# Splitting the inverse products of two chunked mixers over four quadrants of TensorE

## The reference

```python
# gated_delta_chunked, per head and direction, c = 64
a_mat = beta[..., :, None] * jnp.einsum('nhcid,nhcjd->nhcij', k, k) * d_strict
rhs = jnp.concatenate([beta[..., None] * v, (beta * gam)[..., None] * k], axis=-1)
sol = lax.linalg.triangular_solve(a_mat, rhs, left_side=True, lower=True, unit_diagonal=True)
u0, w = sol[..., :dv], sol[..., dv:]
```

## Time and profile before

| | |
|---|---|
| median of 3 runs | 1995.14 us |
| all runs | 2004.53, 1994.45, 1995.14 us |
| span of the profiled execution | 2001.2 us |
| PE busy | 1764.2 us (88%) |
| DVE busy | 857.6 us (43%) |
| ACT busy | 592.7 us (30%) |
| L525 MATMUL (all `product` calls) | 215.5 us busy, 6656 instructions |

### The profile page before, as it was taken

How to read it: one execution, slowest core, us unless ns; L and a number is a source line. 1 busy time by engine, 2 the same in 40 slices (tenths; PEclk the granted TensorE clock), 3 DMA queues, 4 the chain that set the end, 5 groups by cost and what they waited for, 6 DMA issues and landing times.

```text
span 2001.2 us, 44027 instructions
## 1 busy us (share of the span) xinstructions
PE 1764.2 (88%) x17970; PEld 1033.3 (52%) x17970; DVE 857.6 (43%) x1514; ACT 592.7 (30%) x1018; POOL 243.5 (12%) x270
## 2 busy tenths in 40 slices
PE   5998895977778877898999899999989998899996
PEld 2444543544444444445865784354447856853452
DVE  1567524111111111367666753151457747642331
ACT  3314521000000000334324424252253325424442
POOL 0002211111111111006112100001002103000001
PEclk8998996999999999998999999999999999999998
DMA  9758025999999999521000003110211000012101
GB/s 358 259 197 291 1 69 220 370 423 424 423 424 424 425 424 413 216 74 33 3 3 2 3 20 109 42 43 32 80 43 35 3 2 2 4 65 104 42 1 42
DMA packets 75098, 307.75 MB, mean 154 GB/s; under 512 B 10908, under 2 KB 22300, under 8 KB 57888
## 3 DMA queue, kind: packets, MB, share of 16 engines
q1 hardware_dynamic: 63280, 291.98, 37.2%
q0 software_dynamic: 5360, 9.33, 1.3%
q10 hardware_dynamic: 6272, 3.81, 0.6%
HBM read 301.01 MB, written 16.52 MB: 159 GB/s over the span
## 4 chain that ended last, share of the span: by engine, by line
PE 73%; DVE 13%; another core or an unknown queue 6%; ACT 4%; issue 3%; DMA 1%; DVEq 0%; ACTq 0%; POOL 0%; POOLq 0%
PE bank L2253 12%; PE bank L496 12%; PE bank L2269 6%; PE bank L1027 6%; PE bank L525 5%; PE bank L532 4%; PE bank L2091 3%; PE bank L2175 3%; PE bank L998 2%; DVE arena L1596 2%; ACT arena L1039 1%; PE bank L512 1%; PE bank L2115 1%; PE bank L2103 1%
## 5 line engine op out<-in xcount | busy, mean ns | idle before, releaser
L496 PE MATMUL bank<-hT,arena 128*128 128x512 f32 (+1 forms) x640 | 287.7, 605 | 3.6 <-ACTq L1040 2.4
L2253 PE MATMUL bank<-arena 128*64 128x256 f32 x1792 | 216.3, 399 | 66.9 <-remote 66.9
L525 PE MATMUL bank<-arena 64*64 64x64 f32 x6656 | 215.5, 220 | 22.7 <-DVE arena L1726 7.2
L525 PEld LDWEIGHTS bank<-arena 64*64 64x64 f32 x6656 | 203.8, 136 | 37.0 <-DVE arena L1726 10.1
L2253 PEld LDWEIGHTS bank<-arena 128*64 128x64 f32 x1792 | 135.6, 143 | 158.0 <-issue 107.8
L496 PEld LDWEIGHTS bank<-hT,arena 128*128 128x128 f32 (+1 forms) x640 | 122.9, 194 | 161.2 <-issue 156.6
L2859 DVE COPY arena<-bank 128x256 f32<-128x256 f32 x32 | 13.6, 425 | 329.6 <-PE bank L2261 329.6
L2269 PE MATMUL bank<-arena 128*64 128x512 f32 x448 | 104.0, 606 | 16.4 <-remote 16.4
L1027 PE MATMUL bank<-arena 128*128 128x512 f32 x256 | 110.4, 593 | 0.0
L1039 ACT ACTIVATE arena<-bank 128x512 f32<-128x512 f32 (+2 forms) x124 | 73.2, 590 | 118.9 <-PE bank L496 79.2
L532 PE MATMUL bank<-hT,arena 128*128 128x512 f32 x224 | 105.0, 607 | 1.7 <-remote 1.7
(11 more groups left out here) (448 smaller groups left out, 2677.1 us busy)
## 6 DMA issues: line engine op xcount, KB each, us to landing
arena<-w_gate SPq DMA_DIRECT2D x28, 2048.0 KB, 30.6
arena<-w_up SPq DMA_DIRECT2D x28, 2048.0 KB, 21.0
arena<-w_down SPq DMA_DIRECT2D x28, 2048.0 KB, 26.2
arena<-w_ada SPq DMA_DIRECT2D x12, 2048.0 KB, 19.7
arena<-w_in SPq DMA_DIRECT2D x10, 2048.0 KB, 11.7
arena<-w_out SPq DMA_DIRECT2D x6, 2048.0 KB, 7.6
arena<-w_in SPq DMA_DIRECT2D x6, 1536.0 KB, 6.9
hT<-w_up SPq DMA_DIRECT2D x4, 2048.0 KB, 20.9
```

Source lines behind the costliest of these rows:

```text
L496: m = pe.matmul(bank[b][0:w, :], slot2(n)[:, k, c:c + w], hT[:, k, :], start=(k == 0), stop=(k == KD - 1))
L525: m = pe.matmul(o[half(f), s, t], lhs[half(f), s, t], rhs[half(f), s, t], start=True, stop=True)
L2253: mm = pe.matmul(bank[b][c * CAP:(c + 1) * CAP, 0:FE // 2], XT[j][:, k % 4, k // 4, :], e_slot(e_at(e, i), KD)[:, k, c * (FE // 2):(c + 1) ...
```

## The change

The eight matrices of a partition half are now seen as four pairs: `by_parity` splits the 512 columns in 64-column pieces with even (`j=0`) and odd (`j=1`) number, which are even and odd token tiles. Products of even tiles stay as they were. For odd tiles, the first product reads half `f` and writes the *other* half; the second product reads V there, with a copy of Y's odd tiles that ACT has put in that half, and writes back to half `f`. Results of even and odd tiles go to two banks, `2d` and `2d+1`; the first product uses columns 0 to 255 of both, the second columns 256 to 511 (`results`).

```diff
+        Y_odd = [rs[:, 256 * d:256 * d + 256].rearrange("p (a n) -> p a n", n=CG) for d in range(2)]
+        def results(d, part):
+            return banks[:, 2 * d:2 * d + 2, 256 * part:256 * part + 256].rearrange("p j (a n) -> p j a n", n=CG)
+        def by_parity(ap):
+            return ap.rearrange("p (a j n) -> p j a n", j=2, n=CG)
...
+            four = [(j, f) for j in range(2) for f in range(2)]
+            def crossing(o, lhs, rhs):
+                lhs, rhs = by_parity(lhs), by_parity(rhs)
+                for a in range(TT):
+                    for j, f in four:
+                        m = pe.matmul(o[half(f ^ j), j, a], lhs[half(f), j, a], rhs[half(f), j, a], start=True, stop=True)
+                return m
+            def returning(o, Y, Y_odd, V, last):
+                Y, V = by_parity(Y), by_parity(V)
+                for a in range(TT):
+                    for j, f in four:
+                        y = Y_odd[half(1 - f), a] if j else Y[half(f), 0, a]
+                        v = V[half(f ^ j), j, a]
+                        m = pe.matmul(o[half(f), j, a], v if last else y, y if last else v, start=True, stop=True)
+                return m
...
                     for l in range(1, LEVELS):
                         for d in range(2):
+                            if l == 1:
+                                for j in range(2):
+                                    pe.wait_ge(bank_free[2 * d + j], 1)
                             t_full[d].wait()
-                            product(d, g_Bn[d], g_T[d]).then_inc(sem(f"g_v_done{d}"), 1)
+                            crossing(results(d, 0), g_Bn[d], g_T[d]).then_inc(sem(f"g_v_done{d}"), 1)
                         for d in range(2):
                             v_full[d].wait()
-                            y_full[d].wait()
-                            if l == 1:
-                                pe.wait_ge(bank_free[2 + d], 1)
...
+                            y_odd[d].wait(2)
+                            returning(results(d, 1), g_Y[d], Y_odd[d], g_V[d],
+                                      l == LEVELS - 1).then_inc(sem(f"g_t_done{d}"), 1)
...
+            def crossed(y_full, d, l, Y, more=1):
+                z = 1 << l
+                o = (1 if d == 0 else 0) if l < LEVELS - 1 else slice(0, 2)
+                def columns(ap):
+                    return ap.rearrange("p a (g o n) -> p a g o n", o=2, n=z)[:, :, :, o]
+                y_full[d].wait(more)
+                for f in range(2):
+                    act.activation(columns(Y_odd[d][half(1 - f)]), columns(by_parity(Y)[half(f), 1]),
+                                   ACT.Copy).then_inc(sem(f"y_odd_full{d}"), 1)
...
                     for l in range(1, LEVELS):
                         for d in range(2):
+                            if l == 1:
+                                crossed(y_full, d, l, g_Y[d], 2 if ht else 1)
                             v_done[d].wait()
                             if l == 1:
                                 pt_full[d].wait()
-                            act.activation(g_V[d], bank[d], ACT.Copy).then_inc(sem(f"g_v_full{d}"), 1)
+                            act.activation(by_parity(g_V[d]), results(d, 0), ACT.Copy).then_inc(sem(f"g_v_full{d}"), 1)
+                            if l > 1:
+                                crossed(y_full, d, l, g_Y[d])
...
                             if l < LEVELS - 1:
-                                dve.copy_predicated(blocks(g_T[d]), merged(d, l, False), blocks(bank[2 + d])).then_inc(sem(f"g_t_full{d}"), 1)
+                                dve.copy_predicated(by_parity(g_T[d]), merged_parity(d, l, False), results(d, 1)).then_inc(sem(f"g_t_full{d}"), 1)
```

More of the change, by code:

```diff
@@ L542, in decay_rows @@
                         for t, f in pairs_in:
-                            m = pe.matmul(pieces(bank[b + d])[half(f), s, t], g_g[half(f), t, c + s:c + s + 1].to_broadcast([CG, CG]),
+                            m = pe.matmul(pieces(bank[at[d]])[half(f), s, t], g_g[half(f), t, c + s:c + s + 1].to_broadcast([CG, CG]),
                                           const2("cum" + name)[half(f), half(f)], start=True, stop=True)
@@ L565, in gdn_chunks @@
                                                    ("g_t_full", "g_y_full", "g_v_full", "g_uw_free")]
-                rk_full = [Count(pe, sem(f"g_rk_full{d}")) for d in range(2)]
+                rk_full, y_odd = [[Count(pe, sem(f"{n}{d}")) for d in range(2)] for n in ("g_rk_full", "y_odd_full")]
                 kk_free = Count(pe, sem("g_kk_free"))
@@ L694, in rwkv_chunks @@
                 in_full, bt_full, k_free = [Count(pe, sem(n)) for n in ("r_in_full", "r_bt_full", "r_k_free")]
+                y_odd = [Count(pe, sem(f"y_odd_full{d}")) for d in range(2)]
                 for b in range(4, 8):
@@ L1159, in act_second @@
                 w_done = Count(act, sem("g_w_done"))
+                y_full = [Count(act, sem(f"g_y_full{d}")) for d in range(2)]
                 for ht in range(3):
@@ L1166, in act_second @@
                     if ht == 1:
-                        values(2, 3)
+                        values(2, 0)
                         raw(6, 2)
@@ L1262, in act_second @@
                         for d in range(2):
+                            if l == 1:
+                                crossed(y_full, d, l, r_kmt[:, ct, d], 2 if ct else 1)
                             v_done[d].wait()
-                            act.activation(r_kr[:, ct, d, 0], bank[d], ACT.Copy).then_inc(sem(f"g_v_full{d}"), 1)
+                            act.activation(by_parity(r_kr[:, ct, d, 0]), results(d, 0), ACT.Copy).then_inc(sem(f"g_v_full{d}"), 1)
+                            if l > 1:
+                                crossed(y_full, d, l, r_kmt[:, ct, d])
                         if ct == 0 and l in (2, 3):
@@ L1500, in exponents @@
                         e_args[d].wait()
-                        chain(dve.tensor_tensor(pieces(g_V[d]), pieces(bank[b + d]), key_term, ALU.add))
+                        chain(dve.tensor_tensor(pieces(g_V[d]), pieces(bank[at[d]]), key_term, ALU.add))
                         dve.tensor_tensor(blocks(g_V[d]), blocks(g_V[d]), over_blocks(const2("farF" if d == 0 else "farB")),
@@ L1600, in dve_second @@
                             else:
-                                dve.copy_predicated(blocks(g_Y[d]), merged(d, l, True), blocks(bank[2 + d])).then_inc(sem(f"g_y_full{d}"), 1)
+                                dve.copy_predicated(by_parity(g_Y[d]), merged_parity(d, l, True), results(d, 1)).then_inc(sem(f"g_y_full{d}"), 1)
                         if l in (2, 3):
@@ L1725, in dve_second @@
                             if l < LEVELS - 1:
-                                dve.copy_predicated(blocks(Tm), merged(d, l, False), blocks(bank[2 + d])).then_inc(sem(f"g_t_full{d}"), 1)
+                                dve.copy_predicated(by_parity(Tm), merged_parity(d, l, False), results(d, 1)).then_inc(sem(f"g_t_full{d}"), 1)
                                 n_t[d] += 1
@@ L1730, in dve_second @@
                             else:
-                                dve.copy_predicated(blocks(Y), merged(d, l, True), blocks(bank[2 + d])).then_inc(sem(f"g_y_full{d}"), 1)
+                                dve.copy_predicated(by_parity(Y), merged_parity(d, l, True), results(d, 1)).then_inc(sem(f"g_y_full{d}"), 1)
                         if ct == 0 and l in (1, 2):
```

52 lines of the change are left out of this document (24 added, 28 removed).

## The result

The changed kernel takes 2007.45 us (median of 4 runs, 2002.70 to 2010.91) where the kernel before takes 1994.82 in the same comparison: ratio 1.0059, interval 1.0033 to 1.0085. It is slower by 0.6 %. The forecast was 1975, 1967 to 1989.

The account below looks back on a forecast made before the run. PE was taken to bound GDN block 2 and RWKV block 2, DVE RWKV block 1. Levels 8.7 + starts 2.8 - late u 1.6 = 9.9 us a layer, 19.8 for both; 1995.1 - 19.8 = 1975 us, range 1967 to 1989.

Parts of the forecast that it names:

- 2 x 8.7: Levels between first and last merge of five blocks: 8.7 us saved per layer, in two layers.
- The starts: Changed products on four quadrants: matmuls start 14.6 ns apart, so 0.47 us a product.
- The rivals of the floor and of the bank: Products: 25 ns start floor gives 1989 us, shared-bank conflict 1998; 0.14 together with dear copies or DVE.
- crosses Y0 from 2.13: In a new level, ACT copies Y0 across halves from 2.13 to 2.65 us after merge 0.
- The second product of d=0 starts at about 2.75: In a new level, PE starts this product 2.75 us after merge 0; the next merge follows at 3.45.
- a period of 3.45 us: A PE-bound level, merge to merge, falls from 4.29 to 3.45 us.
- a rival for dear copies, 1988 us: ACT's Y copies cost 1.15 us a pair, period about 4.1, forecast time 1988; 0.14 together with floor, bank or DVE.
- No DMA is touched: Listed among things unchanged at no cost: weights for these stages were loaded earlier, and no DMA is touched.
- Starts +2.8: Level 1, ahead of each block's first merge: 2.8 us saved per layer.
- late u -1.6: After the last level, u of d=1 starts 0.4 us later: 1.6 us lost per layer over four blocks.
- The clock, given 0.08: Rival: PE idles between shorter products and its clock falls to half, giving 2015 us; chance 0.08.
- costs little: A clock dip in RWKV's first, DVE-bound block costs little, since PE has over 2 us to spare there.

Follow-up runs that it names:

- e2: Changed kernel without ACT's copies of Y's odd tiles; the second product reads Y in place (result wrong): 1981.14 us, ratio 0.9930.
- e7: Changed kernel with ACT's copies still in its queue, but PE waits only for Y, not for them (result wrong): 1989.75 us, ratio 0.9968.
- e1: Kernel before, products on two quadrants as before, plus ACT's copies of Y's odd tiles and the waits for them: 2023.99 us, ratio 1.0145.
- e9: Changed kernel plus 26 small padding matmuls (104 PE instructions) ahead of each layer's first block: 2003.37 us, ratio 1.0038.
- e5: Changed kernel plus 8 small padding matmuls (32 PE instructions) ahead of each layer's first block: 2022.25 us, ratio 1.0122.
- e12: Changed kernel with 26 padding matmuls a layer, and each block's first level without crossing or copies: 2005.66 us, ratio 1.0046.
- e13: Changed kernel with six blocks' copies on GpSimd, 26 padding matmuls a layer, and first levels without crossing or copies: 2000.04 us, ratio 1.0013.
- e10: Changed kernel with the Y copies of six of ten blocks on GpSimd instead of ACT, plus 26 padding matmuls a layer: 1992.97 us, ratio 0.9984.
- e15: Changed kernel with crossing only in six blocks, copies on GpSimd; the first GDN and first RWKV blocks keep straight products without copies: 1992.35 us, ratio 0.9966.
- e16: Changed kernel with crossing only in six blocks, copies on GpSimd, plus 26 padding matmuls a layer: 1991.40 us, ratio 0.9970.
- e11: Kernel before plus 26 padding matmuls a layer: 2001.26 us, ratio 1.0026.
- e3: Changed kernel plus idle-filling matmuls of 256 columns behind three products of each level from level 2 on: 2007.21 us, ratio 1.0057.
- e6: Changed kernel plus a smaller filler, matmuls of 192 columns behind two products of each level from level 2 on: 2008.58 us, ratio 1.0056.

## Why the prediction was wrong

The miss is 32 us: 1975 forecast, 2007.45 measured. In the spans the levels are 3.5 us longer than in the second profile of the kernel before instead of 17.4 shorter (2 x 8.7), which is 21 us of it; the rest, some 12 us, lies outside them.

- **The starts: right.** The new products' matmuls are 15.4 ns apart (32 in 0.48 us), against 14.6 taken. The shared bank cost nothing, and the 25 ns that the page "TensorE: Matmul & The Clock Gate" of the Trainium skill gives as the least distance is not seen in this pattern either. The rivals of the floor and of the bank fall.
- **"crosses Y0 from 2.13", "The second product of d=0 starts at about 2.75", "a period of 3.45 us": the step that failed, and the one that weighs most.** The sum let the pair of copies end with V1, so that it cost a level nothing: its 3.45 us with copies is no more than e2's 3.42 without. Measured, the product waits for the pair and starts at 3.04 us: V copy to copy 0.63 for 0.50 us, the pair 0.64 for 0.52, to the product 0.14 for 0.10, product to merge 0.75 for 0.70. A clean level is 3.79 us. The pair hardly overlaps: the 0.1 us was taken from V copies of 512 elements. Without copies the run is 26 us faster (e2), and some 18 us of these are the wait for them (e7); on the old products they cost 29 us (e1). The forecast had a rival for dear copies, 1988 us at 1.15 us a pair; the pair was not dear, it stood in the chain.
- **How far this error goes in the levels.** Over the twenty-four intervals of the six PE-bound or mixed blocks 0.34 us each is 8 us, an estimate; by this alone the levels would be 171 us. e9, with 0.6 us of stops left in them, has 172.2. The changed kernel has 183.5, and the 11 us between are stops and clock, which no run separates.
- **"No DMA is touched" (in the sum): the second step that failed.** It left out the DMA that brings PE's own instructions. With 4.3 us for 256 instructions supply kept up; at 3.4 to 4.0 us it stops PE up to once a level unless the boundary falls where PE waits anyway: 7.2 us at least in the levels and 3.6 in the products for w. 32 more instructions made the run 15 us worse (e5).
- **"Starts +2.8", "late u -1.6": no gain between the blocks.** Per layer +1.2 was reckoned, and there it lost 4.5 us. The starts of GDN blocks 2 and 3 won nothing (3.50 us for 3.46), since ACT's pair stands ahead of the V copy. The loss goes with the copies: 9.2 us in e1 without crossing, none in e2 without copies. By what path beyond the first level stays open; e12 and e13 do not tell.
- **The clock, given 0.08:** PEclk is 0.71 in RWKV's first block, where I wrote that a dip "costs little" since DVE bounds it. The block is 0.4 us longer. One interval makes that (4.86 us for 4.39), and it takes 4.85 us in e1 too, at full clock, and 4.42 in e9; so the dip is not shown to be what costs there. Over 50 us more are spent at half clock in the changed kernel. It does not go with the stops (e10 has 2.1 us of them and 85.0 at half clock, e15 6.2 and 38.0); it went with crossing in the first GDN and the first RWKV block: without it there e15 has no more than the kernel before, and e16 (58.4) as much as the kernel before with the same padding (e11, 57.5). How much of the 12.6 us the clock takes by itself stays open: the fillers of e3 and e6 gave back clock and took the same time in instructions.
- **Against the range.** The sum was 19.8 us to win. The same kernel without copies won 14 (e2), so some 6 us were missing even with free copies; its 7 stops, 7.2 us in the levels, are a cause at hand, not shown by a run of its own. Its 1981 us lies inside the range only because the copies that the sum counted are gone.

## What to carry to other kernels

Halving the active time of an engine that bounds a stage moves the bound to what was hidden: here to a copy in the queue of an engine that already stood in the chain, and to the supply of instructions. Put a new helper copy on an engine that is idle at that moment, even if the copy is no faster there, and make the change only in the stages which it shortens. To price such a copy, run the kernel once without it and once with it but with nothing waiting for it. When many tiny instructions run faster than before, look for stops with no releaser that recur at a fixed count of instructions, and before judging a version pad it by a few dozen instructions: two paddings of this one differ by 17 to 19 us.

## What the runs showed of the hardware

- One DMA queue moves 135 packets of 16 KB, and 256 matmuls and weight loads start between two of them in the levels; a stop there ends 2.4 to 2.9 us after a packet's transfer started. No stop in a level at 4.3 us for 256 instructions, up to one a level at 3.4 to 4.0.
- ACT copies 64 x 128 fp32 from one half of the partitions to the other in 0.31 us (0.42 for 64 x 256); GpSimd's fastest in 0.29, 0.35 on average. A pair on ACT takes 0.64 to 0.66.
- Matmuls on four quadrants, two of which write the two partition halves of one bank and two those of another, start 15.4 ns apart on average.
